# A hybrid HGRN2 and Fourier block: the heads' score products in three visits a step from second buffers, and the last head's output taken into the tail

## The chip, the cores and the metric

The kernel runs on one core of a Trainium2 chip. The metric is the device time of one execution in microseconds (us), the median of several runs. PE is the matrix engine, PEld its weight loads, DVE the vector engine, ACT the scalar engine, POOL the general engine, SP the engine that here only issues DMA transfers. A row with a q behind the engine (SPq, ACTq) is that engine's sequencer, for example when it issues a transfer.

## What is computed

One layer of a block over 2048 tokens of width 1024. After a norm with modulation, `h @ w_in` gives seven pieces of 1024 columns. Half of them feed eight heads of a recurrence that runs over the tokens forwards and backwards; the rest goes through a Fourier mixing; `w_out` joins both.

```python
k = (1.0 - lb) * jax.nn.sigmoid(-z);  log_f = jnp.log(jnp.maximum(1.0 - k, F_MIN))
...
o_inter = jnp.einsum("bhtd,bhde->bhte", qc * jnp.exp(bcum), state)
scores = jnp.einsum("bhtd,bhsd,bhtsd->bhts", qc, kc, decay)
o_intra = jnp.einsum("bhts,bhse->bhte", scores, vc)
state = state * jnp.exp(b_end)[:, :, 0, :, None] + jnp.einsum(
    "bhsd,bhse->bhde", kc * jnp.exp(b_end - bcum), vc)
...
o = o_f + flip(o_b)
out = jnp.concatenate([y_a, y_f], axis=-1) @ w_out
```

## The kernel before

Every engine has its own program, written by hand, and works it off in order; semaphores hold the engines together. There are three stages. `front` makes h, h's high and low parts (a product in float32 is three products of such parts, `mm3`, whose lines L61, L62, L63 stand for it everywhere) and the first pieces. `heads` runs eight heads. `tail` does the Fourier mixing and the output product.

In `heads` a head has NG = 4 steps (g = 0 to 3) of 512 tokens, each for both directions d = 0 and 1. Two streams of PE work are interleaved by hand in `step`:

- `project_half(h, g, slot)`, slots 0 to 9: 12 products of 128x512 each, half a tile of a piece for the next head or for this head's gates. In the last two heads only the eight slots 0, 1, 3, 4, 5, 7, 8 and 9 are filled, and in the very last step none is. I call such a half P0 to P9.
- The head's own products. The scores of a 128-token tile are made by levels, each from queries and keys that DVE has scaled for it: the first level within blocks of 8 (L1423), then the pairs of blocks of 8 and 16 (L1439), of 32 and 64 (L1452). Then the keys are transposed (L1462), the increments of the state made (L1469), and the outputs (L1478, L1479; for g = 2 and 3 both lines, for g = 0 and 1 only the second).

So PE's order in a step is P0, first level, P1 P2, level 8, P3, level 16, P4, level 32, P5, level 64, P6 P7, transposes, P8, increments, P9, outputs: the products of a head stand in eight places between halves, five of them for scores.

DVE's order in a step: `clear_scores` (L1573, g = 0 and 1), the scaling for level 8 (L1642 and L1643, with `total` L1646), `copy_scores` and `join_scores`, then for each of LEVELS = (8, 16, 32, 64) the scaling of half of the queries and keys in place (L1666, L1667, L1670) with two parts of `prepare` for the next step behind it (gates; parts 6 and 7 are the reciprocals of L1615). Then `copy_scores` of the last mask, the chain of the state (L1691, L1699), and `first_operands` of the next step (L1623 to L1629). A weight piece for the projections is split by ACT (`split_high`, L1499) and DVE (`split_low`, L1559) at places that `split_due` picks; the first piece of the next head is split after the chain of g = 3. Queries, keys and values lie in two buffers each, and SP's `load` fetches those of the next step when the step before has ended.

All scaling is in place, so DVE can scale for a level only when PE has read the level before, and PE can start a level only when DVE is through.

`tail` starts on PE with `channel_weights(0)`, `middle(0)` and `channels(0)` (L2495 and the three lines of `mm3`), for which DVE folds the loaded waves (`fold_again`, `split_fold_low`, `split_cw_low`) and ACT makes the high parts. Before ACT's first `split_p_high` it waits for the stores of the last outputs, `o_stored`. Later PE wants the third block of the Fourier rows for `f_part(2, 0, F_FIRST)`, which SP fetches by `load_f(2)` behind `load_o(0)`.

Of the kernel before, what the change touches and what calls it, by code (L numbers as in the profile page):

```python
# [35 lines left out]
P = 128  # L36
# [1123 lines left out]
class Leaving:  # L1160
# [12 lines left out]
    steps: int  # L1173


def heads(nc, block, r, front_room, work, spare, bank, handed, w_in, one_minus_lb, ident, masks, h_hi, h_lo, states, value_rows, scratch, o_rows):
# [44 lines left out]
    query = [[piece(f"query{d}{b}", at + d * row) for b, at in enumerate((VALUES + 6 * row, RAW))] for d in range(2)]  # L1221
    key = [[piece(f"key{d}{b}", at + d * row) for b, at in enumerate((HC + 6 * row, RAW + 2 * row))] for d in range(2)]
# [8 lines left out]
    score = [tiles(f"score{g}", spare + g * row) for g in range(NG)]  # L1231
# [8 lines left out]
    loaded = [[r.sem(f"loaded{d}{b}") for b in range(2)] for d in range(2)]  # L1240
    near_cleared, score_cleared = r.sem("near_cleared"), r.sem("score_cleared")
# [9 lines left out]
    key_t_copied = [r.sem(f"key_t_copied{d}") for d in range(2)]  # L1251
    o_copied = [r.sem(f"o_copied{d}") for d in range(2)]
# [3 lines left out]
    LOADS = 3  # L1256
# [15 lines left out]
    def ordered(ap, d, b):  # L1272

        return in_time(ap, d).rearrange("p (n two b) -> p n two b", two=2, b=b)

# [21 lines left out]


# [29 lines left out]
    def _(sp):  # L1328
# [5 lines left out]
        def load(h, g, parts=("key", "value", "query")):  # L1334
            for d in range(2):
                t = group_of(d, g) * GRP
                sem, b = loaded[d][g % 2], g % 2
                if "key" in parts:
                    sp.dma_start(key[d][b][:], scratch[key_names[d]][bass.ds(h * P, P), t:t + GRP]).then_inc(sem, DMA)
# [3 lines left out]
                if "query" in parts:  # L1343
                    sp.dma_start(query[d][b][:], scratch["query"][bass.ds(h * P, P), t:t + GRP]).then_inc(sem, DMA)

        def first_loads():
# [13 lines left out]
            load(0, 1, ("key", "query"))  # L1360
            sp.wait_ge(handed.product, handed.all_fills)
            load(0, 1, ("value",))
# [4 lines left out]
        def turn(h, last):  # L1367
            if h:
                start_state(h)
            for g in range(0 if h else 1, NG):  # L1370
                if g == NG - 1 and last:
                    break
                for d in range(2):
                    wait_count(sp, product[d], PROD * (NG * h + g))
                if g < NG - 1:
                    load(h, g + 1)
                else:
                    for b in range(2):
                        wait_count(sp, proj_stored[b], (FIRST_UNIT[h] // 2 + 6) * DMA)
                    load(h + 1, 0)  # L1380
# [7 lines left out]
    def _(pe):  # L1388
# [22 lines left out]
        def tile(ap, t):  # L1411
            return ap[:, t * P:(t + 1) * P]

        def step(h, g, last):
            n, b = NG * h + g, g % 2
            project_half(h, g, 0)
            for d in range(2):
                wait_count(pe, loaded[d][b], (2 * h + g // 2 + 1) * LOADS * DMA)
                wait_count(pe, operand[d], OPS * n + 1)
                for t in range(TPG):  # L1420
                    for part in PARTS:
                        for half, keys in enumerate((first_half[d], key[d][b])):
                            done = nc.tensor.matmul(half_block(ps[d][0][part, t, part], d, half), tile(keys, t)[:, part],  # L1423
                                                    half_block(tile(query[d][b], t)[:, part], d, half), start=True, stop=True)
# [1280 lines left out]
```

## Time and profile before

| | us |
|---|---|
| median of 3 runs | 2205.48 (2204.68 to 2206.7) |
| the profiled execution | 2205.83, its span 2204.1 |
| PE busy | 2114.9 |
| DVE busy | 1531.6 |
| ACT busy | 508.3 |
| heads on PE: first L1423 to last L1479 | 515.6 to 1684.4 |

The span runs from the first to the last instruction, and busy is the time in which an engine had work in it. A PE instruction is shown from its start to the end of its pipeline, so the next one starts before it ends: what a run of products costs is the distance between the starts of its first row and of the next run's first row.

### The profile page before, as it was taken

To read this page: it belongs to the slowest core of one execution; us is meant where nothing else is said; L and a number is where in the kernel's file an instruction comes from. 1 tells how busy PE (TensorE), PEld (TensorE's weight loads), DVE (VectorE), ACT (ScalarE), POOL (GpSimd) and SP (SyncE) were. 2 spreads that over 40 slices of the span, in tenths; PEclk is the share of its full clock that TensorE was granted. 3 is DMA by queue.
4 is the path that set the end of the run, shared out by engine and by line. 5 is a ranking of instruction groups with operands and counts; after the bars stand their busy time and mean duration, and the time that the engine had idled before them with its cause. 6 is when DMAs were issued, how large, how long until landed. Compare 5 with 4: busy or idle time off the path is not lost.

```text
span 2204.1 us, 48217 instructions
## 1 busy us (share of the span) xinstructions
PE 2114.9 (96%) x20564; PEld 1776.8 (81%) x20564; DVE 1531.6 (69%) x3275; ACT 508.3 (23%) x836; POOL 75.0 (3%) x109
## 2 busy tenths in 40 slices
PE   5899999999999999999999999999996999999997
PEld 3799988788788788888887887877776887888886
DVE  5865854026777878787787778798896886555554
ACT  3711133111112111212121122111112343212121
POOL 0001101000000000000000000000000010000000
PEclk9999999999999999999999999999997999999999
DMA  8444555342424333333334243333335366534451
GB/s 316 159 131 144 183 156 155 120 132 74 130 83 132 106 115 100 117 111 98 117 94 135 83 132 96 110 112 116 103 103 193 139 229 231 196 127 162 149 177 57
DMA packets 229863, 298.89 MB, mean 136 GB/s; under 512 B 14934, under 2 KB 159990, under 8 KB 226322
## 3 DMA queue, kind: packets, MB, share of 16 engines
q1 hardware_dynamic: 145346, 178.38, 25.1%
q10 hardware_dynamic: 73952, 81.18, 10.8%
q0 software_dynamic: 10352, 36.25, 5.1%
q8 instruction: 163, 2.67, 0.5%
q14 instruction: 50, 0.41, 0.1%
HBM read 198.16 MB, written 97.59 MB: 134 GB/s over the span
## 4 chain that ended last, share of the span: by engine, by line
PE 88%; DVE 5%; DMA 2%; issue 1%; ACT 1%; SPq 1%; ACTq 0%; POOL 0%; DVEq 0%
PE all_bank L61 25%; PE all_bank L63 23%; PE all_bank L62 23%; PE all_bank L1479 3%; PE all_bank L1469 2%; PE all_bank L1423 2%; PE all_bank L1439 2%; PE all_bank L1452 1%; PE all_bank L1462 1%; PE all_bank L1478 1%; DVE hidden_h_lo L483 1%; DMA front_w_mod<-in_w_ada 1%; SPq L366 1%; PE all_bank L1008 1%; PE all_bank L2566 1%
## 5 line engine op out<-in xcount | busy, mean ns | idle before, releaser
L61 PE MATMUL all_bank<-hidden_h_hi,head_hi 128*128 128x512 f32 x1184 | 491.0, 415 | 2.2 <-issue 2.2
L63 PE MATMUL all_bank<-hidden_h_hi,head_lo 128*128 128x512 f32 x1184 | 465.4, 393 | 0.0
L62 PE MATMUL all_bank<-hidden_h_lo,head_hi 128*128 128x512 f32 x1184 | 463.1, 391 | 0.0
L1515 ACT ACTIVATE head_projected<-all_bank 128x512 f32<-128x512 f32 x148 | 88.6, 599 | 864.2 <-PE all_bank L63 864.2
L63 PEld LDWEIGHTS all_bank<-hidden_h_hi,head_lo 128*128 128x128 f32 x1184 | 222.6, 188 | 51.8
L61 PEld LDWEIGHTS all_bank<-hidden_h_hi,head_hi 128*128 128x128 f32 x1184 | 222.9, 188 | 47.4 <-issue 2.5
L62 PEld LDWEIGHTS all_bank<-hidden_h_lo,head_hi 128*128 128x128 f32 x1184 | 223.4, 189 | 41.7 <-issue 2.0
L1615 DVE RECIPROCAL head_inverse<-head_gate 128x448 f32<-128x448 f32 x64 | 185.8, 2930 | 0.0
L1666 DVE TENSOR_TENSOR head_query<-head_query,head_total 128x256 f32<-128x256 f32 x256 | 107.8, 421 | 81.9 <-PE all_bank L1439 51.4
L61 PE MATMUL all_bank<-front_hi,hidden_h_hi 128*128 128x256 f32 x512 | 143.8, 281 | 0.0
L63 PE MATMUL all_bank<-front_hi,hidden_h_lo 128*128 128x256 f32 x512 | 142.7, 279 | 0.0
L62 PE MATMUL all_bank<-front_lo,hidden_h_hi 128*128 128x256 f32 x512 | 142.6, 279 | 0.0
L1667 DVE TENSOR_TENSOR head_key<-head_key,head_total 128x256 f32<-128x256 f32 x256 | 107.3, 419 | 0.0
L61 PE MATMUL all_bank<-tail_w_hi,tail_f_hi 128*128 128x512 f32 x256 | 100.6, 393 | 3.1 <-DVE tail_f_lo L2138 3.1
L61 PE MATMUL all_bank<-tail_w_hi,tail_a_hi 128*128 128x512 f32 x256 | 101.4, 396 | 1.1 <-DVE tail_a_lo L2171 1.1
L63 PE MATMUL all_bank<-tail_w_hi,tail_f_lo 128*128 128x512 f32 x256 | 100.4, 392 | 0.0
L62 PE MATMUL all_bank<-tail_w_lo,tail_f_hi 128*128 128x512 f32 x256 | 100.3, 392 | 0.0
L63 PE MATMUL all_bank<-tail_w_hi,tail_a_lo 128*128 128x512 f32 x256 | 99.9, 390 | 0.0
L62 PE MATMUL all_bank<-tail_w_lo,tail_a_hi 128*128 128x512 f32 x256 | 99.7, 389 | 0.0
L61 PEld LDWEIGHTS all_bank<-front_hi,hidden_h_hi 128*128 128x128 f32 x512 | 96.9, 189 | 0.5 <-issue 0.4
L1642 DVE TENSOR_TENSOR head_query<-head_query,head_gate 128x512 f32<-128x512 f32 x64 | 43.6, 681 | 76.8 <-PE all_bank L1423 76.8
L63 PEld LDWEIGHTS all_bank<-front_hi,hidden_h_lo 128*128 128x128 f32 x512 | 96.5, 188 | 0.0
(294 smaller groups left out, 4151.4 us busy)
## 6 DMA issues: line engine op xcount, KB each, us to landing
head_raw<-in_w_in POOLq DMA_DIRECT2D x37, 512.0 KB, 4.8
head_value<-value_rows SPq DMA_DIRECT2D x64, 256.0 KB, 5.2
head_query<-piece_query SPq DMA_DIRECT2D x64, 256.0 KB, 6.7
head_out<-head_o ACTq DMA_DIRECT2D x64, 256.0 KB, 6.1
tail_o<-head_out SPq DMA_DIRECT2D x32, 512.0 KB, 5.9
front_raw<-in_w_in SPq DMA_DIRECT2D x19, 512.0 KB, 5.1
front_stage<-in_x SPq DMA_DIRECT2D x16, 512.0 KB, 6.9
front_w_mod<-in_w_ada SPq DMA_DIRECT2D x8, 1024.0 KB, 13.6
```

Source lines behind the costliest of these rows:

```text
L61: nc.tensor.matmul(out, st_hi, mv_hi, start=start, stop=False)
L62: nc.tensor.matmul(out, st_hi, mv_lo, start=False, stop=False)
L63: return nc.tensor.matmul(out, st_lo, mv_hi, start=False, stop=stop)
L1423: done = nc.tensor.matmul(half_block(ps[d][0][part, t, part], d, half), tile(keys, t)[:, part], half_block(tile(query[d][b], t)[:, part], ...
L1439: done = nc.tensor.matmul(meeting(ps[d][BANK_OF[i]][part, t, part], d, LEVELS[i]), tile(key[d][b], t)[:, part], meeting(tile(query[d][b], ...
L1469: done = nc.tensor.matmul(ps[d][1][:, t, :], key_t[d][:, t, :], value[d][b][:, t, :], start=True, stop=True)
L1479: done = nc.tensor.matmul(ps[d][2][:, t, :], tile(query[d][b], t), state[d][:, before, :], start=g < NG // 2, stop=True)
L1515: nc.scalar.activation(projected[unit % 2][:], ps_proj[unit % 2][:], PIECES[name][1], scale=PIECES[name][2]).then_inc(proj_copied, 1)
L1615: nc.vector.reciprocal(in_blocks(inverse[d][:], d)[:, :, 1:BASE], in_blocks(gate[d][:], d)[:, :, 1:BASE]).then_inc(gated[d], 1)
L1642: nc.vector.tensor_tensor(qs, qs, f[:, :, 0:1].to_broadcast([P, GRP // BASE, BASE]), ALU.mult)
L1666: nc.vector.tensor_tensor(qs[:, :, 1, :], qs[:, :, 1, :], tot[:, :, 0, :].to_broadcast(shape), ALU.mult)
L1667: nc.vector.tensor_tensor(ks[:, :, 0, :], ks[:, :, 0, :], tot[:, :, 1, :].to_broadcast(shape), ALU.mult).then_inc(operand[d], 1)
```

## The change

In `heads`:

- Queries and keys lose their second buffer (`query[d]`, `key[d]`). The scaling for level 8 goes out of place into new tiles `query_far`, `key_far`, planes of `query_planes` and `key_planes`, by `far_operands`, which DVE runs at the end of the step before, right behind `first_operands`. Levels 8 and 16 scale these in place as before; the step to level 64 is written into the other planes (`query_turned`, `key_turned`), so it needn't wait for PE to read level 32; the step behind level 64 writes back, and four small copies on ACT (`returned`) bring back what it leaves.
- PE does the scores in three visits: first level and level 8, then level 16 behind P1 P2, then levels 32 and 64 behind P3 P4; P5 P6 P7 follow. Level 64 is made by 16 products of 32 by 64 in place of 8 of 64 by 64.
- DVE's order is changed with it, and `split_due` puts pieces due at slots 7 to 9 behind both reciprocals.
- SP issues a step's two key loads first, on semaphores of their own (`key_here`). It does so when the first level has been read and `far_operands` is through, so inside the step before.
- The last step's chain, outputs and output copies (`chain`, `outputs`, `rows_out`) are called from `tail`: the chain behind DVE's three clearing operations, the outputs behind `channel_weights(0)`, the copies behind ACT's splits of the channel weights.

In `tail`: ACT waits for `o_stored` only before the fifth `split_p_high`; `load_f(2)` is issued before `load_o(0)`, and `split_f_low(2)` comes before `add_directions(0)`.

```diff
-    query = [[piece(f"query{d}{b}", at + d * row) for b, at in enumerate((VALUES + 6 * row, RAW))] for d in range(2)]
+    query = [piece(f"query{d}", VALUES + (6 + d) * row) for d in range(2)]
...
+                    if after is not None:
+                        wait_count(sp, product[d], PROD * after + 1)
+                        wait_count(sp, operand[d], OPS * after + 2)
+                    sp.dma_start(key[d][:], scratch[key_names[d]][bass.ds(h * P, P), t:t + GRP]).then_inc(key_here[d], DMA)
...
-            project_half(h, g, 1)
-            project_half(h, g, 2)
             if n == 0:
                 pe.wait_ge(handed.evacuated, handed.all_fills)
...
+            level_in_parts(n, 0)
+            for slot in range(1, 3):
+                project_half(h, g, slot)
+            level_in_parts(n, 1)
+            for slot in range(3, 5):
+                project_half(h, g, slot)
...
+            for t in range(TPG):
+                for side in range(2):
+                    for d in range(2):
+                        done = nc.tensor.matmul(ps[d][2][PARTS[2 * d + side], t, (1 - d) * 64:(2 - d) * 64], joint_key(d)[:, 2 * t + d, side, :],
+                                                joint_query(d)[:, 2 * t + 1 - d, :, :], start=True, stop=True)
...
+                wait_count(pe, returned[d], 2 * (n + 1))
...
-                if (step, max(1, min(slot - 2, 4))) == (g, level):
+                if (step, 1 if slot < 3 else 2 if slot < 5 else 5 if slot > 6 else 4) == (g, level):
...
+        def far_operands(h, g):
+            n = NG * h + g
+            for d in range(2):
+                qs, ks, q_far, k_far, f = (in_blocks(ap, d) for ap in (query[d][:], key[d][:], query_far[d], key_far[d], gate[d][:]))
+                wait_count(v, product[d], PROD * n)
+                wait_count(v, operand[d], OPS * n + 1)
+                nc.vector.tensor_tensor(q_far, qs, f[:, :, 0:1].to_broadcast([P, GRP // BASE, BASE]), ALU.mult)
+                nc.vector.tensor_tensor(k_far, ks, f[:, :, BASE - 1:BASE].to_broadcast([P, GRP // BASE, BASE]), ALU.mult
+                                        ).then_inc(operand[d], 1)
...
             for d in range(2):
+                next_level(n, d, 0)
...
+            prepare_next(1, (0, 1))
+            for i in (1, 2):
                 for d in range(2):
...
+                    next_level(n, d, i)
+            prepare_next(2, (2, 3))
+            prepare_next(3, (4, 5))
+            for d in range(2):
+                next_level(n, d, 3)
+            prepare_next(4, (6, 7))
...
             if not ends:
                 first_operands(*next_step(h, g))
+                far_operands(*next_step(h, g))
...
+        left.chain(v, HEADS - 1, NG - 1)
...
-            sp.wait_ge(left.o_stored[d], left.steps * DMA)
+        load_f(2)
         load_o(0)
-        load_f(2)
...
+                if n == 0 and f == 4:
+                    for d in range(2):
+                        act.wait_ge(left.o_stored[d], left.steps * DMA)
                 split_p_high(n, f)
...
         channel_weights(0)
+        left.outputs(pe, HEADS - 1, NG - 1)
```

PE's order in one full step before, the first row of each run of like products (`head_query` and `head_key` are DVE's scaled operands; rows of L61 begin the projections):

```order
L1423 MATMUL all_bank6<-head_query00_5600,head_first_half0_5616 32x4x4 [waits head_operand0,head_loaded00]
...
L61 MATMUL all_bank4<-hidden_h_hi0_51,head_hi0_5594 128x512
...
L1439 MATMUL all_bank0<-head_query00_5600,head_key00_5604 32x2x8 [waits head_chained0,head_operand0]
...
L61 MATMUL all_bank5<-hidden_h_hi1_52,head_hi0_5594 128x512
...
L1439 MATMUL all_bank2<-head_query00_5600,head_key00_5604 32x16 [waits head_o_copied0,head_operand0]
...
L61 MATMUL all_bank4<-hidden_h_hi2_53,head_hi0_5594 128x512 [waits head_proj_copied]
...
L1452 MATMUL all_bank2<-head_query00_5600,head_key00_5604 32x32 [waits head_operand1,head_operand0]
...
L61 MATMUL all_bank4<-hidden_h_hi2_53,head_hi0_5594 128x512
...
L1452 MATMUL all_bank2<-head_query00_5600,head_key00_5604 64x64 [waits head_operand1,head_operand0]
...
L61 MATMUL all_bank5<-hidden_h_hi3_54,head_hi0_5594 128x512 [waits head_proj_copied]
...
L1462 MATMUL all_bank6<-all_ident,head_key00_5604 128x128 [waits head_copied0,head_operand0]
```

And the same place after the change:

```order
L1510 MATMUL all_bank6<-head_query0_5600,head_first_half0_5616 32x4x4 [waits head_operand0,head_loaded00]
...
L1497 MATMUL all_bank0<-head_query_planes0_5604,head_key_planes0_5606 32x2x8 [waits head_chained0,head_operand0]
...
L61 MATMUL all_bank4<-hidden_h_hi0_51,head_hi0_5594 128x512
...
L1497 MATMUL all_bank2<-head_query_planes0_5604,head_key_planes0_5606 32x16 [waits head_o_copied0,head_operand0]
...
L61 MATMUL all_bank5<-hidden_h_hi1_52,head_hi0_5594 128x512
...
L1527 MATMUL all_bank2<-head_query_planes0_5604,head_key_planes0_5606 32x32 [waits head_operand1,head_operand0]
...
L1536 MATMUL all_bank2<-head_query_planes0_5604,head_key_planes0_5606 32x64 [waits head_operand1,head_operand0]
...
L61 MATMUL all_bank4<-hidden_h_hi2_53,head_hi0_5594 128x512
...
L1547 MATMUL all_bank6<-all_ident,head_key_planes0_5606 128x128 [waits head_returned0,head_copied0,head_operand0]
```

The five separate places of score products have become three; L1536 is level 64, and the transposes of L1547 wait for ACT's `returned` as well.

DVE's order from the last operation of `first_operands` (L1629) into the next step, before (a step with g = 2, where nothing is cleared):

```order
L1629 TENSOR_TENSOR head_key10_5606<-head_key10_5606,head_inverse1_5615 128x64x4
L1642 TENSOR_TENSOR head_query00_5600<-head_query00_5600,head_gate0_5612 128x512 [waits head_operand0,head_product0]
L1643 TENSOR_TENSOR head_key00_5604<-head_key00_5604,head_gate0_5612 128x512
L1646 TENSOR_TENSOR head_total0_5622<-head_gate0_5612 128x64 [waits head_copied0]
L1642 TENSOR_TENSOR head_query10_5602<-head_query10_5602,head_gate1_5613 128x512 [waits head_operand1,head_product1]
L1643 TENSOR_TENSOR head_key10_5606<-head_key10_5606,head_gate1_5613 128x512
L1646 TENSOR_TENSOR head_total1_5623<-head_gate1_5613 128x64 [waits head_copied1]
L1589 COPY_PREDICATED head_near0_5624<-hidden_masks_49,all_bank6 128x512
...
L1666 TENSOR_TENSOR head_query00_5600<-head_query00_5600,head_total0_5622 128x32x8 [waits head_totalled0,head_operand0,head_product0]
```

And after the change, where L1706 is that last operation and L1714 and L1715 are `far_operands`:

```order
L1706 TENSOR_TENSOR head_key1_5603<-head_key1_5603,head_inverse1_5615 128x64x4
L1714 TENSOR_TENSOR head_query_planes0_5604<-head_query0_5600,head_gate0_5612 128x512 [waits head_operand0,head_product0]
L1715 TENSOR_TENSOR head_key_planes0_5606<-head_key0_5602,head_gate0_5612 128x512
L1719 TENSOR_TENSOR head_total0_5622<-head_gate0_5612 128x64 [waits head_copied0,head_chained0]
L1714 TENSOR_TENSOR head_query_planes1_5605<-head_query1_5601,head_gate1_5613 128x512 [waits head_operand1,head_product1]
L1715 TENSOR_TENSOR head_key_planes1_5607<-head_key1_5603,head_gate1_5613 128x512
L1719 TENSOR_TENSOR head_total1_5623<-head_gate1_5613 128x64 [waits head_copied1,head_chained1]
L1731 TENSOR_TENSOR head_query_planes0_5604<-head_query_planes0_5604,head_total0_5622 128x32x8 [waits head_totalled0,head_operand0,head_product0]
L1732 TENSOR_TENSOR head_key_planes0_5606<-head_key_planes0_5606,head_total0_5622 128x32x8
```

The scaling for level 8 stays right behind `first_operands` in DVE's order, but it now waits for the outputs of the step before instead of PE's first level of this step. The scaling for level 16 (L1731) now comes ahead of the first `copy_scores`.

SP's transfers for one step before:

```order
L1339 DMA head_key00_5604<-piece_key_f 128x512 [waits head_proj_stored0,head_proj_stored1,head_product1,head_product0]
L1341 DMA head_value00_5608<-value_rows 128x4x128
L1344 DMA head_query00_5600<-piece_query 128x512
L1339 DMA head_key10_5606<-piece_key_b 128x512
L1341 DMA head_value10_5610<-value_rows 128x4x128
L1344 DMA head_query10_5602<-piece_query 128x512
```

And after:

```order
L1417 DMA head_key0_5602<-piece_key_f 128x512 [waits head_product0,head_operand0,head_proj_stored1,head_proj_stored0]
L1417 DMA head_key1_5603<-piece_key_b 128x512 [waits head_operand1,head_product1]
L1422 DMA head_value00_5608<-value_rows 128x4x128
L1425 DMA head_query0_5600<-piece_query 128x512
L1422 DMA head_value10_5610<-value_rows 128x4x128
L1425 DMA head_query1_5601<-piece_query 128x512
```

Both keys now come first, and each waits for DVE's and PE's use of the one buffer.

## Rows read from the trace of the kernel before

**Rows 1.** The page: busy time by engine, and the chain that ended last by engine.

```profile
PE 2114.9 (96%) x20564; PEld 1776.8 (81%) x20564; DVE 1531.6 (69%) x3275; ACT 508.3 (23%) x836; POOL 75.0 (3%) x109
...
PE 88%; DVE 5%; DMA 2%; issue 1%; ACT 1%; SPq 1%; ACTq 0%; POOL 0%; DVEq 0%
```

**Rows 2.** Windows: stretch, length, busy us of each engine, granted clock, DMA share, GB/s.

```profile
1100.00:1200.00 100.00, 99.03 (x1199) 81.49 (x1199) 78.56 (x195) 19.71 (x30) 3.54 (x4) 1.00 0.34 105
1600.00:1700.00 100.00, 82.19 (x1163) 68.58 (x1161) 80.20 (x215) 17.21 (x33) 0.10 (x1) 0.89 0.39 134
1692.00:1696.00 4.00, 4.00 (x19) 3.85 (x19) 1.36 (x3) 0.82 (x3) 0.00 (x0) 0.50 1.03 427
```

**Rows 3.** Timeline of PE, third head, g = 1: start, us, instruction, count.

```profile
856.79 0.26 PE L1423 MATMUL all_bank<-head_query,head_first_half 128*32 128x16 f32 x7
...
858.18 0.50 PE L61 MATMUL all_bank<-hidden_h_hi,head_hi 128*128 128x512 f32 x1
...
863.87 0.74 PE L1439 MATMUL all_bank<-head_query,head_key 128*32 128x16 f32 x64
...
871.11 0.46 PE L1452 MATMUL all_bank<-head_query,head_key 128*32 128x32 f32 x32
871.50 0.50 PE L61 MATMUL all_bank<-hidden_h_hi,head_hi 128*128 128x512 f32 x1
...
874.46 0.69 PE L1452 MATMUL all_bank<-head_query,head_key 128*64 128x64 f32 x16
875.08 0.50 PE L61 MATMUL all_bank<-hidden_h_hi,head_hi 128*128 128x512 f32 x1
```

**Rows 4.** Timeline of PE, the same step's last projection run and its outputs.

```profile
886.03 0.48 PE L61 MATMUL all_bank<-hidden_h_hi,head_hi 128*128 128x512 f32 x1
...
890.02 1.24 PE L1479 MATMUL all_bank<-head_state,head_query 128*128 128x128 f32 x9 [0.97 <-DVE head_state L1699]
```

**Rows 5.** Timeline of DVE, the same step: a wait inside it.

```profile
883.04 1.23 DVE L1559 TENSOR_TENSOR head_lo<-head_raw,head_hi 128x1024 fp32r<-128x1024 f32 x1 [3.42 <-ACT head_hi L1499]
```

**Rows 6.** Timeline of DVE, third head, from g = 0 into g = 1.

```profile
848.75 0.35 DVE L1699 SCALAR_TENSOR_TENSOR head_state<-head_state,head_total,all_bank 128x128 f32<-128x128 f32 x1 [1.60 <-issue]
...
854.33 0.43 DVE L1629 TENSOR_TENSOR head_key<-head_key,head_inverse 128x256 f32<-128x256 f32 x1
...
857.66 0.69 DVE L1642 TENSOR_TENSOR head_query<-head_query,head_gate 128x512 f32<-128x512 f32 x1 [1.82 <-PE all_bank L1423]
...
860.27 0.27 DVE L1646 TENSOR_TENSOR head_total<-head_gate 128x64 f32<-128x64 f32 x1
```

**Rows 7.** Timeline of DVE, from the sixth head into the seventh.

```profile
1424.43 1.23 DVE L1559 TENSOR_TENSOR head_lo<-head_raw,head_hi 128x1024 fp32r<-128x1024 f32 x1 [2.96 <-ACT head_hi L1499]
...
1428.45 0.43 DVE L1629 TENSOR_TENSOR head_key<-head_key,head_inverse 128x256 f32<-128x256 f32 x1
```

**Rows 8.** Timeline of PE: starts of the first level in heads seven and eight.

```profile
1428.67 0.26 PE L1423 MATMUL all_bank<-head_query,head_first_half 128*32 128x16 f32 x7
...
1463.79 0.26 PE L1423 MATMUL all_bank<-head_query,head_first_half 128*32 128x16 f32 x7
...
1495.07 0.26 PE L1423 MATMUL all_bank<-head_query,head_first_half 128*32 128x16 f32 x7
...
1660.56 0.26 PE L1423 MATMUL all_bank<-head_query,head_first_half 128*32 128x16 f32 x7
```

**Rows 9.** DMA issues: queue, count, KB each, median us from issue to landing.

```profile
head_key<-piece_key_b SPq DMA_DIRECT2D x32, 256.0 KB, 5.9
```

**Rows 10.** Timeline of PE at the start of the tail and at its third Fourier block.

```profile
1690.94 0.38 PE L2475 MATMUL all_bank<-tail_cw,tail_mid_in 128*1 128x256 f32 x1 [3.67 <-DVE tail_cw_lo L2089]
...
1701.63 0.58 PE L61 MATMUL all_bank<-tail_cw_hi,tail_fold_hi 128*128 128x256 f32 x1 [4.00 <-DVE tail_mid_lo L2094]
...
1840.76 0.47 PE L61 MATMUL all_bank<-tail_w_hi,tail_f_hi 128*128 128x512 f32 x1 [2.81 <-DVE tail_f_lo L2138]
```

**Rows 11.** Timeline of ACT at the start of the tail.

```profile
1700.76 0.37 ACT L2385 ACTIVATE tail_mid_hi<-all_bank 1x256 fp32r<-1x256 f32 x1 [7.83 <-issue]
```

More of the change, by code:

```diff
@@ L1255, in heads @@
     key_names = ("key_f", "key_b")
-    LOADS = 3
+    LOADS = 2
     def meeting(ap, d, size):
@@ L1458, in step @@
+            for slot in range(5, 8):
+                project_half(h, g, slot)
             for d in range(2):
@@ L1471, in step @@
             project_half(h, g, 9)
-            for d in range(2):
-                wait_count(pe, copied[d], MASKED * n + MASKED)
-                wait_count(pe, chained[d], CHAIN * n + TPG)
-                for t in range(TPG):
-                    before = t if d == 0 else TPG - 1 - t
-                    if g >= NG // 2:
-                        nc.tensor.matmul(ps[d][2][:, t, :], score[group_of(d, g)][:, t, :], value[d][b][:, t, :], start=True, stop=False)
-                    done = nc.tensor.matmul(ps[d][2][:, t, :], tile(query[d][b], t), state[d][:, before, :], start=g < NG // 2, stop=True)
-                done.then_inc(product[d], 1)
+            if not (last and g == NG - 1):
+                outputs(pe, h, g)
         pe.wait_ge(handed.sig_done, HEADS)
@@ L1649, in step, with prepare_next @@
                 v.wait_ge(handed.masks_in, DMA)
+            def prepare_next(level, parts):
+                due = split_due(h, g, level)
+                if not ends:
+                    prepare(*next_step(h, g), parts[0])
+                if due is not None:
+                    split_low(h, due)
+                if not ends:
+                    prepare(*next_step(h, g), parts[1])
             for d in range(2):
+                next_level(n, d, 0)
+            for d in range(2):
+                wait_count(v, product[d], PROD * n + 1)
                 if g < NG // 2:
@@ L2378, in _ @@
         nc.scalar.activation(sign_row[:], raw_sign_row[:], ACT.Copy).then_inc(signs_ready, 1)
-        for d in range(2):
-            act.wait_ge(left.o_stored[d], left.steps * DMA)
         for n in range(FG):
@@ L2389, in _ @@
             for f in range(8):
+                if n == 0 and f == 2:
+                    for sem in left.proj_stored:
+                        act.wait_ge(sem, left.all_units // 2 * DMA)
+                if n == 0 and f == 4:
+                    for d in range(2):
+                        act.wait_ge(left.o_stored[d], left.steps * DMA)
                 split_p_high(n, f)
```

281 lines of the change are left out of this document (168 added, 113 removed).

## The prediction

> **What bounds the kernel now.** I read the page first. PE is busy for 2114.9 of 2204.1 us and makes up 88% of the chain that ended last, DVE 5% [rows 1]. So only what shortens PE's own stream, or an idle stretch of it, counts. The windows say where idle time is: in a hundred microseconds of the middle heads PE is busy for 99.03, in the hundred that end the heads for 82.19, at a mean granted clock of 0.89 [rows 2]. So in the middle heads the change can gain only by cheaper PE work, and at the end by removed waits too.
>
> The timeline of PE shows what a visit costs. A lone half of 12 products between two visits takes 874.46 - 871.50 = 2.96 us; two halves in a row take 863.87 - 858.18 = 5.69 [rows 3]. From 2.96 and 5.69, a half that only lengthens a run costs 2.73, and each break adds about 0.22.
>
> The same timeline has one wait that recurs: at g = 1 of heads one to six the projections ahead of the outputs take 890.02 - 886.03 = 3.99 us, because PE waits for the chain of the state [rows 4]. DVE is late there since it stood 3.42 us for ACT's high part of a weight piece, with one reciprocal still to do [rows 5].
>
> In heads seven and eight, with eight halves a step, DVE becomes the limit. The seven steps before the last take 1660.56 - 1428.67 = 231.9 us. The second, which has no PE wait at its scores, takes 1495.07 - 1463.79 = 31.28 [rows 8].
>
> **The change part by part.**
>
> *Fewer visits.* Of the runs P1 P2, P3, P4, P5, P6 P7 (2 x 5.69 + 3 x 2.96 = 20.26) there remain P1 P2, P3 P4, P5 P6 P7: 5.69 + 5.69 + 8.42 = 19.80. Two breaks fewer: 0.44 a step after rounding down. I take 0.44 x 31 = 13.6 us; the last step has no halves. That more work in a row saves nothing bounds it at 0.
>
> *Level 64.* It takes 875.08 - 874.46 = 0.62 us for 16 rows of 64x64; afterwards 32 rows with 32 columns of weights and 64 moving. Level 32, with the same number of rows and the same 32-column weights but half the moving columns, takes 871.50 - 871.11 = 0.39 [rows 3]. So the new level 64 lies between 0.39 and twice that, 0.78: from 0.23 gained to 0.16 lost a step. Four column groups now run side by side as in level 32, so I take 0.52, a gain of 0.1, 3 us in all, with -5 to +7 as ends.
>
> The first level shows the pace of small products: 128 rows in 858.18 - 856.79 = 1.39 us, 10.9 ns each [rows 3]. The Trainium skill, "TensorE: Matmul & The Clock Gate", section "Part 1: The HAM clock gate", says that the start-to-start distance never drops below about 25 ns however few columns there are. By that 32 rows would take 0.8 us, and level 64 would lose 0.18 a step, 5.6 us in all. The row is less than half of that floor here, so the measurement decides.
>
> *The wait at g = 1.* The piece that waits for ACT now comes behind both reciprocals. DVE then loses only what exceeds them (2.9 us of the 3.42 are covered), and before the chain it has 1.60 us to spare at g = 0 [rows 5, 6]. So the six waits go: 3.99 - 2.96 = 1.03 each, 6 us.
>
> *Level 8 right behind the first level.* Its cover, P1 P2, is gone; what is late next is `far_operands`. At g = 0 DVE ends the last operation of `first_operands` at 854.76, 2.03 before PE's first level at 856.79 [rows 3, 6]. `far_operands` is L1642 to L1646 for both directions: 860.54 - 857.66 = 2.9 us [rows 6]. Started at 854.7 it ends at 857.5, while the second direction's level 8 is wanted at 856.79 + 1.39 + 0.3 = 858.5. That leaves about 0.9 of cover, more at g = 2, where the outputs are 32 rows and not 16. If this cover is missing, each microsecond costs one at every step.
>
> It is missing at the seven boundaries between heads. There DVE waits 2.96 us for ACT before it splits the next weight piece, and ends `first_operands` at 1428.88 [rows 7]; `far_operands` would follow to 1431.8, its last key operand to about 1431.6. PE starts the first level at 1428.67 [rows 8] and would want the second level 8 at 1430.4, 1.2 earlier. That is a new loss of 7 x 1.2 = 8, less 1 that level 8 waits there already: 7 us lost.
>
> *Heads seven and eight.* With no waits, the seven steps would take four times 31.28, three times 33.2 (two microseconds more for the double outputs), less 2.96 because the last of them is not followed by P0: 221.8. So 10 us are waits for level 8, whose operands DVE makes too late. They are ready early now. DVE's own work is some 28.5 us a step, so it follows closely. I leave 2 us for levels 32 and 64, which are now wanted together. Gain 8, between 4 and 10; the boundaries' loss is booked above.
>
> *Keys.* They are fetched inside the step: SP issues about 0.8 and 1.4 us after the first level starts. The second key's median landing is 5.9 us behind two other transfers [rows 9], with one ahead I take 4.6. So both are there 6 us into the step, when DVE has cleared, scaled level 16 and copied twice. Behind DVE's wait for them stand the scalings for levels 32 and 64. With ten halves level 64 is wanted at 14.3, and key plus two parts, a weight split and two scalings need 6.1 us: 2 us of cover. With eight halves it is wanted at 11.8, and 5.0 are needed: 0.8 of cover. Cost nothing. ACT's four copies lie under P5 P6 P7.
>
> *Last step and tail.* In the last step PE only follows DVE and ACT. Its order saves about a microsecond. The chain's tail end then lies under `channel_weights(0)`. PE's `middle(0)` waited 3.67 us at 1690.94 for folds that DVE started behind the chain, with ACT busy with the output copies ahead of its splits; both come earlier now. `channels(0)` then stood 4.00 us up to 1701.63, because ACT had waited 7.83 us for stores to land before its first high part [rows 10, 11]. That wait moves to the fifth part. Meanwhile PE worked at a granted clock of 0.50, which is its 1.2 GHz level [rows 2]. Sum of 1 + 3.67 + 4.00 is 8.7; the stores may still be late for the fifth part, so I take 8, from 3 (only the first wait) to 11 (with time back from the clock).
>
> *Third Fourier block.* PE waited 2.81 us [rows 10]. Its load is issued three transfers earlier; but the first heads' rows then land later, and the turning of heads follows. 2.5 gained, 0 to 3.
>
> **Sum.** 13.6 + 3 + 6 - 7 + 8 + 8 + 2.5 = 34.1 us off the profiled 2205.83, which is 0.35 above the median 2205.48. Off the median it gives 2171.4, and I say 2171.
>
> **The rivals.**
> - *Forecast,* 2171, own range 2160 to 2182.
> - *The cover of level 8 is not there at g = 0 to 2 either.* If `far_operands` ends 1 us later than the 0.9 of cover allows, 24 further steps lose 1 each: 2171 + 24 = 2195. For it: DVE's chain hardly moves while PE's step shrinks. Against it: at g = 0 DVE still waits 1.60 us before the chain [rows 6].
> - *Breaks cost what they did,* since level 8 and the longer runs bring their own start-up: no 13.6, so 2185. Against it are the two runs of [rows 3].
> - *Small products keep to a floor.* Level 64 then takes 0.8: 2171 + 3 + 5.6 = 2180.
> - *Slower: late keys.* If the second key landed 8.9 us after its issue, 3 above the median, it would be there 10.3 into the step. Level 64 is then late by 2.1 in 12 steps, by 1 in 12 without a split, and by 3.5 in 7 of eight halves: 25 + 12 + 25 = 62, so 2233. It outweighs the gain from about 7.5 us after issue on. For it: one buffer, and the output stores are in flight. Against it: the median, and that keys go first.
>
> **How the numbers follow.** Forecast 0.64; level 8 exposed 0.14; breaks not saved 0.09; floor 0.03; late keys 0.06; the gains just eaten up by small losses in several places 0.04. The range 2158 to 2193 takes in the first, third and fourth, and a part of the second (the cover missed by less). A difference under 0.2%, 4.4 us, can't be told from no change here. Faster: 0.64 + 0.14 + 0.09 + 0.03, less 0.01, is 0.89; same 0.04; slower 0.07.
>
> **What would show it.** After: two halves in a row at 5.7 and P5 P6 P7 at 8.4 us; level 64 at 0.5; no 3.99 at g = 1; a PE wait of some 1.2 before level 8 only where a head begins; DVE's first part of `prepare` hardly waiting for keys; `middle(0)` some 5 us sooner after the last step's first level, and no 4 us wait in `channels(0)`. The prediction is wrong if waits at level 8 stand in every step, if L1673 waits for DMA for more than 2 us, or if PE's wait for `f_part(2, 0, F_FIRST)` only moves to the heads' turning.

## The result and the profile after

| | before | after |
|---|---|---|
| median, side by side | 2206.19 us (2204.68 to 2208.93) | 2212.14 us (2206.21 to 2218.65) |
| runs | 8 | 8 |
| the profiled execution, its span | 2205.83, 2204.1 | 2210.46, 2208.7 |

The ratio is 1.0029, with a 95% interval of 1.0015 to 1.0043. The kernel became slightly slower. The forecast was 2171, so some 40 us are missing.

The page after answers to [rows 1]:

```profile
PE 2105.5 (95%) x21076; PEld 1784.5 (81%) x21076; DVE 1531.3 (69%) x3275; ACT 537.2 (24%) x964; POOL 74.9 (3%) x109
...
PE 87%; DVE 5%; issue 3%; DMA 2%; ACT 2%; SPq 1%; ACTq 0%; DVEq 0%
```

PE's busy time fell by 9.4 us and the span rose by 4.6. The share "issue", time in which PE waited for nothing that the profile shows, rose from 1% to 3%. DVE and DMA kept theirs, ACT went from 1% to 2%.

I read the timeline of PE in several steps of the changed kernel. This is the third head's g = 2, it answers to [rows 3] (L1497 is level 8, then level 16; L1527 is level 32, L1536 level 64; the first level began 1.27 us earlier). Each float32 product of the code's levels stands there as two rows, and the counts in this text are of rows:

```profile
868.23 0.74 PE L1497 MATMUL all_bank<-head_query_planes,head_key_planes 128*32 128x16 f32 x63
868.89 0.51 PE L61 MATMUL all_bank<-hidden_h_hi,head_hi 128*128 128x512 f32 x1
...
874.61 0.74 PE L1497 MATMUL all_bank<-head_query_planes,head_key_planes 128*32 128x16 f32 x64
875.28 0.51 PE L61 MATMUL all_bank<-hidden_h_hi,head_hi 128*128 128x512 f32 x1
...
881.00 0.46 PE L1527 MATMUL all_bank<-head_query_planes,head_key_planes 128*32 128x32 f32 x32
881.27 0.68 PE L1536 MATMUL all_bank<-head_query_planes,head_key_planes 128*32 128x64 f32 x32
881.88 0.50 PE L61 MATMUL all_bank<-hidden_h_hi,head_hi 128*128 128x512 f32 x1
...
890.24 1.04 PE L1547 MATMUL all_bank<-all_ident,head_key_planes 128*128 128x128 f32 x8
```

Here all is as planned. Two halves in a row take 874.61 - 868.89 = 5.72, three take 890.24 - 881.88 = 8.36. Levels 32 and 64 together take 881.88 - 881.00 = 0.88, against 0.39 + 0.62 = 1.01 in [rows 3]. Level 8 follows the first level without a pause.

In about half the steps something else happens. Three of them:

```profile
980.68 0.25 PE L1497 MATMUL all_bank<-head_query_planes,head_key_planes 128*32 128x16 f32 x7
984.34 0.95 PE L1497 MATMUL all_bank<-head_query_planes,head_key_planes 128*32 128x16 f32 x57 [3.41 <-issue]
985.22 0.80 PE L61 MATMUL all_bank<-hidden_h_hi,head_hi 128*128 128x512 f32 x1
985.81 0.63 PE L62 MATMUL all_bank<-hidden_h_lo,head_hi 128*128 128x512 f32 x1
...
1025.51 0.45 PE L1497 MATMUL all_bank<-head_query_planes,head_key_planes 128*32 128x16 f32 x32 [1.92 <-issue]
...
1103.99 0.40 PE L61 MATMUL all_bank<-hidden_h_hi,head_hi 128*128 128x512 f32 x1 [1.86 <-issue]
```

Level 8 is 64 rows, and its semaphores are waited for ahead of each direction's 32. PE stopped for 3.41 us behind the 7th row, where the code has no wait at all, and elsewhere behind the last one. There it can be no late operand. Ahead of its last step the heads' stage has 15 such stops in the changed kernel. From the start of the product ahead to the start of the one behind they last 1.38 to 3.59 us, 35.7 in all. The longest also slow what follows, as the windows show (columns as in [rows 2]):

```profile
984.00:986.00 2.00, 1.66 (x59) 1.53 (x59) 1.07 (x4) 0.00 (x0) 0.00 (x0) 0.50 0.92 279
986.00:988.00 2.00, 2.00 (x7) 1.52 (x6) 2.00 (x6) 0.00 (x0) 0.00 (x0) 0.50 0.92 296
988.00:990.00 2.00, 2.00 (x6) 1.60 (x5) 1.24 (x4) 0.00 (x0) 0.00 (x0) 0.50 0.06 18
```

After the pause the granted clock is 0.50, the 1.2 GHz level, and the next two halves take 8.2 us instead of 5.7. So they do behind the stops at 517.30, 670.64 and 1291.42 as well (8.1 to 8.3 us).

The expected wait where a head begins, and the tail:

```profile
832.03 0.45 PE L1497 MATMUL all_bank<-head_query_planes,head_key_planes 128*32 128x16 f32 x32 [0.94 <-DVE head_key_planes L1715]
...
1702.82 0.59 PE L2591 MATMUL all_bank<-tail_cw,tail_mid_in 128*1 128x256 f32 x2 [1.13 <-DVE tail_cw_lo L2199]
1710.01 0.35 PE L61 MATMUL all_bank<-tail_cw_hi,tail_fold_hi 128*128 128x256 f32 x1 [0.65 <-DVE tail_p_lo L2209]
...
1826.64 0.50 PE L61 MATMUL all_bank<-tail_w_hi,tail_f_hi 128*128 128x512 f32 x1 [0.67 <-DVE tail_f_lo L2248]
```

The boundary wait is 0.94 us of idle time, and 1.1 us from start to start (I had said 1.2). The waits of 3.67, 4.00 and 2.81 us of [rows 10] are 1.13, 0.65 and 0.67 now.

**What the stops share.** PE's instructions come by a DMA queue of their own. The page has it before and after (packets, MB, share of the span):

```profile
q8 instruction: 163, 2.67, 0.5%
```

```profile
q8 instruction: 167, 2.74, 0.5%
```

I counted PE's instructions in the program, a weight load and a product for each row, and one more for each wait that is an instruction of its own: 41,814 before and 42,838 after. Divided by 163 and 167 packets that is 256.5 in each. So PE is fed in blocks of 256. I then numbered the instructions and looked up the first one behind each stop (seven of the 15 are shown):

```
after:  at us     stop   number   mod 256      before: at us     stop   number   mod 256
        517.30    3.23    7106    194                  1433.54   2.51   30146    194
        670.64    2.82   10946    194                  1499.95   2.34   31938    194
        712.68    1.71   11971    195                  1568.15   2.35   33730    194
        750.78    2.12   12995    195                  1633.13   1.78   35522    194
        980.75    3.59   18882    194
       1101.94    2.04   21954    194
       1617.62    1.96   35522    194
```

All 15 of after and all 4 of before stand at 194 to 196 modulo 256: a block's end. In the trace the packet that ends such a stop starts 2.2 to 2.8 us ahead of its end.

This gives **theory 1**. The next block is asked for about when PE enters one, and takes some microseconds to come: at the 15 stops of after, 3.0 to 5.1 us lie between PE's first instruction of a block and its first one of the next, at the 4 of before 6.1 to 6.6. The first level is 256 instructions in 1.3 us, level 8 is 128 in 0.67. Put back to back, they can hold a whole block, which is used up in 1.3 us. The blocks' ends drift by 16 to 52 instructions a step in heads one to six, therefore some steps stop and others don't. **Theory 2**: VectorE's `far_operands` are late and the profile misattributes it. **Theory 3**: the key, value and query loads, now issued just then, hold something up.

Theory 1 needs one correction, which the same trace gives. PE used up six other blocks of the changed kernel in 1.2 to 2.5 us, from 630.3, 941.1, 1212.6, 1251.8, 1483.0 and 1677.9 on, and stopped for 0.7 us at most at their ends. This is the second of them, the first level's 256 instructions and level 8 behind them without a pause:

```profile
941.08 0.26 PE L1510 MATMUL all_bank<-head_query,head_first_half 128*32 128x16 f32 x7
...
942.47 0.73 PE L1497 MATMUL all_bank<-head_query_planes,head_key_planes 128*32 128x16 f32 x64
```

If the packets carry the blocks in order, the packet with the next block had started 2.2 to 2.9 us ahead of PE's first instruction of the block in five of the six (0.03 behind it in the last). At the 15 stops it started 0.6 to 2.6 us behind that instruction. The 15 blocks begin 10 to 137 instructions behind a step's first small product; of the six, one begins 6 behind it and the others with it or up to 11 ahead. So the next block isn't always asked for when PE enters one: what counts is how long ahead its packet starts. In none of the nine traces does PE begin a block less than 2.2 us behind the start of its packet.

The Trainium skill, "Runtime: NRT & Kernel Launch", section "Instruction fetch mechanics", states that an engine's instruction memory is refilled in 16 KiB blocks of 256 instructions and calls the cost of crossing such a boundary mostly hidden. The block size agrees with the 256.5 counted here. That it is hidden holds for most of this program, but not for these 35.7 us.

### The profile page after: what moved, and what is told of

It reads as the page before. It is cut to its first block, busy times and chain, and to the rows that moved or that the text cites. A ratio compares the mean times of both kernels' runs of the same rounds, so it can differ in the third digit from the quotient of the medians.

```text
span 2208.7 us, 49593 instructions
## 1 busy us (share of the span) xinstructions
PE 2105.5 (95%) x21076; PEld 1784.5 (81%) x21076; DVE 1531.3 (69%) x3275; ACT 537.2 (24%) x964; POOL 74.9 (3%) x109
## 4 chain that ended last, share of the span: by engine, by line
PE 87%; DVE 5%; issue 3%; DMA 2%; ACT 2%; SPq 1%; ACTq 0%; DVEq 0%
PE all_bank L61 25%; PE all_bank L63 24%; PE all_bank L62 23%; PE all_bank L1554 3%; PE all_bank L1345 2%; PE all_bank L1497 2%; PE all_bank L1510 2%; PE all_bank L1547 1%; PE all_bank L1344 1%; DVE hidden_h_lo L483 1%; PE all_bank L1536 1%; PE all_bank L1008 1%; PE all_bank L2682 1%; DMA front_w_mod<-in_w_ada 1%; SPq L366 1%
## 5 line engine op out<-in xcount | busy, mean ns | idle before, releaser
L61 PE MATMUL all_bank<-hidden_h_hi,head_hi 128*128 128x512 f32 x1184 | 488.3, 412 | 2.8 <-issue 2.8
L63 PE MATMUL all_bank<-hidden_h_hi,head_lo 128*128 128x512 f32 x1184 | 470.4, 397 | 0.3 <-issue 0.2
L61 PEld LDWEIGHTS all_bank<-hidden_h_hi,head_hi 128*128 128x128 f32 x1184 | 226.1, 191 | 47.5 <-issue 0.7
L61 PE MATMUL all_bank<-front_hi,hidden_h_hi 128*128 128x256 f32 x512 | 143.6, 281 | 0.0
L1372 DVE SCALAR_TENSOR_TENSOR head_state<-head_state,head_total,all_bank 128x128 f32<-128x128 f32 x256 | 71.8, 343 | 85.8 <-issue 72.1
L1731 DVE TENSOR_TENSOR head_query_planes<-head_query_planes,head_total 128x256 f32<-128x256 f32 x128 | 53.8, 420 | 75.8 <-PE all_bank L1497 60.3
L61 PE MATMUL all_bank<-tail_w_hi,tail_a_hi 128*128 128x512 f32 x256 | 102.1, 399 | 3.0 <-DVE tail_a_lo L2281 3.0
L61 PE MATMUL all_bank<-tail_w_hi,tail_f_hi 128*128 128x512 f32 x256 | 99.9, 390 | 0.7 <-DVE tail_f_lo L2248 0.7
L61 PEld LDWEIGHTS all_bank<-front_hi,hidden_h_hi 128*128 128x128 f32 x512 | 96.7, 189 | 0.5 <-issue 0.4
L62 PEld LDWEIGHTS all_bank<-front_lo,hidden_h_hi 128*128 128x128 f32 x512 | 96.2, 188 | 0.0
```

Source lines behind the costliest of these rows:

```text
L61: nc.tensor.matmul(out, st_hi, mv_hi, start=start, stop=False)
L62: nc.tensor.matmul(out, st_hi, mv_lo, start=False, stop=False)
L63: return nc.tensor.matmul(out, st_lo, mv_hi, start=False, stop=stop)
L1372: nc.vector.scalar_tensor_tensor(state[d][:, j + 1, :], state[d][:, j, :], total_of(d, P)[:, j:j + 1], ps[d][1][:, t, :], ALU.mult, ALU.ad ...
L1731: nc.vector.tensor_tensor(qs, qs, tot[:, :, 0, :].to_broadcast(shape), ALU.mult)
```

## The experiments

**1 and 2. The same program, with its blocks' ends moved.** Waits that are met since long before are instructions as well. Put between projection products they make each step a multiple of 256 long. Nothing is left out or reordered.

```diff
+        def fill(h, g, n, k):
+            first = sum(map(len, SLOTS_OF[h][:g])) + 2
+            places = 4 * (len(SLOTS_OF[h][g]) - 2)
+            at = 4 * (n - first) + k % 4
+            if at >= 0:
+                few = FILL[NG * h + g] * (at + 1) // places - FILL[NG * h + g] * at // places
+                for _ in range(few + 1 if few else 0):
+                    pe.wait_ge(lo_done, 1)
...
             for k in range(half * KT // 2, (half + 1) * KT // 2):
+                fill(h, g, n, k)
                 done = mm3(nc, ps_proj[unit % 2][:], ...
```

The two kernels have the same `FILL` except for step 0, whose entry is 479 in the first and 240 in the second. `FILL` counts calls of `wait_ge`, and by the traces two calls make one instruction: step 0 has 255 instructions more than in the changed kernel in the first and 128 in the second. That sets where a block ends in the later steps: 185 to 191 or 56 to 62 instructions behind the first small product.

> The changed kernel with waits that are always met added ahead of TensorE's projection products, so that every step of the heads holds a multiple of 256 TensorE instructions and the places 194 mod 256 of its program fall about 185 instructions behind each step's first small product (step 0 excepted). Theory 1, TensorE's instructions arrive in blocks of 256 and a block that is used up in under some 4 us leaves it without the next: the stalls of 1.7 to 3.6 us between two products of L1497 go, except that of step 0; 35.7 less 3.2 us of stalls and about 8 us of halved clock behind the longest: 2171 us. Theory 2, VectorE's operands for level 8 come late: nothing in the data's order is changed, the stalls stay, 2212 us. Theory 3, the loads that SyncE now issues just there hold something up: the same, 2212 us.

Measured: 2177.03 us (4 runs), ratio to before 0.9863, interval 0.985 to 0.9877.

> As the first of this set, with 127 to 129 added waits fewer in step 0 and the same ones in every later step, so that the places 194 mod 256 fall about 62 instructions behind each step's first small product. Theory 1: a block of 256 lies wholly in the first level and level 8 in each of the 31 steps behind step 0, each stalls about 2.1 us as the steps with such an offset did in the changed kernel: 2171 + 31 x 2.1 = 2236 us, with all stalls at one place of the step. Theories 2 and 3: no difference to the first of this set, 2212 us or the time that it has.

Measured: 2274.67 us (4 runs), ratio 1.0314, interval 1.0294 to 1.0333. The groups of level 8 and 16 in the two, first the one with the good place:

```profile
L1509 PE MATMUL all_bank<-head_query_planes,head_key_planes 128*32 128x16 f32 x4096 | 49.1, 185 | 12.2 <-DVE head_key_planes L1727 6.6 <-issue 5.0 <-DVE head_key_planes L1744 0.6
```

```profile
L1509 PE MATMUL all_bank<-head_query_planes,head_key_planes 128*32 128x16 f32 x4096 | 57.2, 188 | 70.2 <-issue 69.7 <-DVE head_key_planes L1744 0.3
```

The idle time put down to "issue" is 5.0 us in one and 69.7 in the other. Three steps of the second:

```profile
845.99 0.75 PE L1509 MATMUL all_bank<-head_query_planes,head_key_planes 128*32 128x16 f32 x37 [3.32 <-issue]
...
886.43 0.57 PE L1509 MATMUL all_bank<-head_query_planes,head_key_planes 128*32 128x16 f32 x37 [1.81 <-issue]
...
1374.23 0.57 PE L1509 MATMUL all_bank<-head_query_planes,head_key_planes 128*32 128x16 f32 x37 [1.97 <-issue]
```

In these, 37 rows of level 8 are left each time. Every step from 1 to the last stops at a number of 194 or 195 modulo 256. Data, order of the work, operands and loads are the same in both kernels, which lie 98 us apart. That rules theories 2 and 3 out as the cause and bears theory 1 out. I had put the bad one 39 us too low. The 32 stops make 78.9 us, 2.5 each and not 2.1. In 12 steps of heads one to six the next two halves took 6.95 to 8.23 us instead of 5.7, where I had counted no clock at all:

```profile
846.00:850.00 4.00, 4.00 (x45) 3.29 (x45) 3.67 (x11) 0.00 (x0) 0.00 (x0) 0.50 0.82 259
```

The good one missed 2171 by 6 us, in step 0: it took 47.1 us there, with a stop of 3.45, then the clock at half, and 255 added waits to pay for.

**3. The kernel before with filled steps.** The same `fill`.

> The kernel before with the same filling of its steps, places 194 mod 256 about 185 behind each step's first small product. Theory 1: its four stalls between products of level 8 in heads 7 and 8 (2.51, 2.34, 2.35 and 1.78 us at 1433.54, 1499.95, 1568.15 and 1633.13) go, 9.0 us: 2197 us. Theory 2, these four are waits for VectorE, as the prediction booked them: 2206 us. Against the first of this set it tells what the rest of the change is worth when neither kernel stalls for instructions: 26 us by theory 1.

Measured: 2212.0 us, ratio 1.002, interval 1.0011 to 1.0029: a miss, by 15 us. The stops of 2.3 us in level 8 of heads seven and eight did go. This is one in the kernel before, then two of what stands in the filled one:

```profile
1436.05 0.18 PE L1439 MATMUL all_bank<-head_query,head_key 128*32 128x16 f32 x1 [2.32 <-issue]
```

```profile
1440.86 0.47 PE L61 MATMUL all_bank<-hidden_h_hi,head_hi 128*128 128x512 f32 x1 [0.72 <-issue]
...
1474.37 0.47 PE L61 MATMUL all_bank<-hidden_h_hi,head_hi 128*128 128x512 f32 x1 [0.87 <-issue]
```

The block's end now falls into the projections behind level 8, with only 2.9 us of them between the two levels, and steps there stop for up to 1.3 us from start to start, where before every second one stopped for 1.8 to 2.5. In these seven steps PE's idle time put down to "issue" is 5.2 us in all, and 3.7 more are waits for ACT's copies of the projections, which before didn't have. The filling costs too: heads one to six, which had no long stop, take 3.3 us more in all, and the part from the last step on 3.2 more, for which I have no cause. So four stops of before were waits for instructions, not for VectorE, but filling alone gives nothing back there.

**4. The part behind the heads alone.** The last step's outputs, rows and chain in the stage behind, its splits and loads in the new order, on the kernel before:

```diff
             project_half(h, g, 9)
-            for d in range(2):
-                wait_count(pe, copied[d], MASKED * n + MASKED)
...
+            if not (last and g == NG - 1):
+                outputs(pe, h, g)
```

> The kernel before with the part of the change behind the last head alone (the last step's outputs, rows and chain moved into the stage behind, the order of its splits and loads). If the gain there is independent of the heads, it is the 12 us by which the stretch from the last step's first level to the end is shorter in the changed kernel: 2194 us. If that gain depends on the new buffers or on what the heads leave behind: between 2194 and 2206 us.

Measured: 2194.6 us, ratio 0.9946, interval 0.9933 to 0.9958. This part gives 12 us by itself.

**5. Level 8 behind slots 1 and 2 again,** with nothing filled:

```diff
-            level_in_parts(n, 0)
             for slot in range(1, 3):
                 project_half(h, g, slot)
+            level_in_parts(n, 0)
+            project_half(h, g, 3)
             level_in_parts(n, 1)
-            for slot in range(3, 5):
-                project_half(h, g, slot)
+            project_half(h, g, 4)
```

> The changed kernel with level 8 behind slots 1 and 2 again, slot 3 behind level 8, slot 4 behind level 16, nothing filled up: four visits to the scores instead of three. Theory of the instruction blocks: 5.7 us of projections lie between the 256 instructions of the first level and the 128 of level 8 in heads 1 to 6, so the 40 us of stalls and halved clock there go; heads 7 and 8, with 2.9 us between, keep some of what the kernel before had (up to 9 us); one visit more costs 31 x 0.22 = 7 us, and the waits of 0.94 us at the seven boundaries of heads go, 7 us: 2212 - 40 + 9 + 7 - 7 = 2181 us. If the three visits were worth nothing, the time is no longer than the 2177 us of the filled three visits.

Measured: 2251.81 us, ratio 1.02, interval 1.0179 to 1.0221: a miss of 71 us. The stops for instructions are nearly gone, but a real wait took their place:

```profile
898.06 0.46 PE L1527 MATMUL all_bank<-head_query_planes,head_key_planes 128*32 128x32 f32 x32 [0.89 <-DVE head_key_planes L1732]
899.57 0.65 PE L1536 MATMUL all_bank<-head_query_planes,head_key_planes 128*32 128x64 f32 x31 [1.05 <-DVE head_key_planes L1737]
```

By groups, level 32 stood 26.8 us for VectorE and level 64 stood 31.6. The clock takes its part too: in 12 steps the three halves behind level 64 took 9.4 to 10.1 us instead of 8.4, some 18 us in all, with windows like this one:

```profile
900.00:904.00 4.00, 4.00 (x26) 3.10 (x16) 4.00 (x14) 0.91 (x4) 0.00 (x0) 0.57 0.02 5
```

In the changed kernel both are wanted 5.7 us behind level 16, here 3.0. Level 8 right behind the first level is what makes room for two halves between the others. It can't be moved back alone.

**6 and 7. The filled kernel with step 0 put right.** The front's last products get met waits as well, so that in step 0 a block ends 192 instructions behind the first small product. In the second, heads seven and eight use other slots:

```diff
+FRONT_FILL = [4, 4, 4, 4, 4, 4, 3, 3]
...
                 for k in range(KT):
+                    if n == NB - 1 and f >= 2:
+                        for _ in range(FRONT_FILL[k]):
+                            pe.wait_ge(lo_done, 1)
                     last = mm3(nc, bank[n_fill % 4][:, u * W:(u + 1) * W], a_hi[:, k, at], a_lo[:, k, at],
```

```diff
-    EIGHT = (0, 1, 3, 4, 5, 7, 8, 9)
+    EIGHT = (0, 1, 2, 3, 5, 7, 8, 9)
```

> The changed kernel filled to 256 in every step, as the run that took 2177 us, and 196 or so met waits added to the last products of the front too, so that step 0 has its block's end at 192 as well and needs no 255 of them itself. Theory of the instruction blocks: the stall of 3.45 us in step 0 goes and some 7 us of halved clock and of filling there: 2167 us. If step 0's loss was due to the start of the stage: 2177 us.

Measured: 2168.63 us, ratio 0.9824, interval 0.9809 to 0.984. Step 0 takes 36.1 us instead of 47.1.

> As the run before it, with the eight slots of heads 7 and 8 as 0, 1, 2, 3, 5, 7, 8, 9 instead of 0, 1, 3, 4, 5, 7, 8, 9: 24 projection products behind level 8 and 12 behind level 16. Theory of the instruction blocks: the stalls of about 1 us behind level 8 in heads 7 and 8 (three in the first filled run) go: 3 us less than the run before it, 2164 us. Against it: VectorE must have level 32 and 64 ready behind 2.9 us of projections instead of 5.7, and is late: slower than the run before it by up to 7 x 2 us.

Measured: 2166.75 us, ratio 0.9822, interval 0.9808 to 0.9837: no difference to the run before it that these runs can tell. The short stops in heads seven and eight went ("issue" idle 0.3 us there instead of 1.0), and level 64 waited for VectorE five times there, 0.9 us in all, where it had not waited before. Both kernels beat the two given ones by about 40 us. One stop is left in each, in the last step, which has no projections (the second's):

```profile
1641.99 0.75 PE L1515 MATMUL all_bank<-head_query_planes,head_key_planes 128*32 128x16 f32 x34 [4.64 <-issue]
```

PE's stretches, from first products to first products, in us:

| | step 0 | rest of heads 1 to 6 | heads 7, 8 but the last step | from the last step on |
|---|---|---|---|---|
| before | 36.8 | 876.3 | 231.9 | 543.5 |
| changed | 41.7 | 894.9 | 226.4 | 530.3 |
| 1, good place | 47.1 | 859.2 | 222.8 | 534.8 |
| 2, bad place | 39.5 | 933.1 | 247.6 | 535.3 |
| 6 | 36.1 | 859.3 | 222.3 | 532.9 |

## Why the prediction was wrong

**The step that failed** is "Level 8 right behind the first level". I asked there whether DVE would have the operands in time, and priced PE's small products by their pace alone. How PE's own instructions reach it was no term of the sum. The change put 384 of them into 2.0 us. That cost 35.7 us of stops and some 12 of halved clock behind them. Ahead of the last step the changed kernel's heads took 1163.0 us and those of experiment 6 1117.7, 45.3 less, its added waits included. This turned the gain of 34 into a loss of 6. Experiments 1 and 2 show it: the same work at the good place is 35 us faster than the changed kernel, at the bad place 63 slower.

**A reading that failed** is "Heads seven and eight". I took all of the 10 us above the pace of a step without waits as level 8 waiting for DVE. The rows say "<-issue", in the middle of a run of products. Four stops make up 9.0 of them, and all four stand at a block's end. That the term of 8 came out close (231.9 to 222.3 in experiment 6, 9.6) is luck, since its reason was wrong. The warning stood in the profile of before: the two levels with only 2.9 us between them stopped 2.3 us, in heads seven and eight alone. I should have asked what these steps have that others lack.

**Terms that held.** They can be read once the stops are gone, in experiment 6:
- Visits: two halves at 5.7, three at 8.4; 0.46 a step, 0.44 as put.
- Level 64: 0.13 a step with level 32, forecast 0.1. The rival's 0.8 us for the 32 rows didn't come: they took 0.61 us, 19 ns each.
- g = 1: the wait is gone in all six heads.
- Boundaries: 0.94 us idle and 1.1 from start to start, where I had 1.2. The first level is also 0.1 us shorter in each step, 3 to 4 us in all, which I hadn't counted.
- Heads in all: 1145.0 before, 1117.7 in experiment 6, 27.3 gained. The sum had 23.6 (34.1 less 8 and 2.5). Of the 27.3, 17.7 lie in heads one to six and 9.6 in seven and eight.
- Last step and tail: 12 us alone (experiment 4), forecast 10.5.

With its instructions in time the change takes 2168.6 us, near the 2171 of the forecast. Part of this nearness is luck too: 9.0 us of the gain are the kernel before's own four stops, which the sum had under another name.

**The rivals.** The cover of level 8, breaks and the floor did not come true. The late keys did not either: in the changed kernel `prepare` (L1673) waited 3.7 us for keys in all, of which 2.9 were ahead of the first step and 0.8 inside the heads. Level 64 stood for VectorE once, for 0.8 us, in the last step, which has no projections. By its letter one sign of being wrong was met, a wait of L1673 for DMA above 2 us; the wait of 2.1 lies at 484.2, 31 us ahead of PE's first level of the first head. "Slower" had 0.07 of the chance, and none of that lay on the mechanism that made it slower.

## What to carry to other kernels

- Count TensorE's instructions as well as their time. In experiment 2 a block of 256 lay wholly in small products in all 31 steps behind step 0, and all 31 stopped. With some 4 us of work in a block, four steps of heads seven and eight of the kernel before stopped and others of the same kernel didn't. And blocks that began just ahead of the small products were used up in 1.2 to 2.5 us without a long stop. So look at where in the stretch a block begins. Keeping the two short runs apart by long products cost more here (experiment 5); moving the blocks' ends by filling paid off in the changed kernel (1 and 6), not in the one before (3).
- "<-issue" in the middle of a run whose code has no wait there is a reading of its own. Look at the distance from start to start and at the instruction's number in the program before you book it as a late operand.
- If a change makes some steps slower and their equals not, compare where in the program, not only in the step, they stand.

## What the runs showed of the hardware

- TensorE's instructions arrived in blocks of 256 (163 packets for 41,814, 167 for 42,838). The stops ended 2.2 to 2.8 us behind the start of their packet, and in all nine traces no block was begun sooner than that behind its packet's start, if packets carry blocks in order. Between PE's first instruction of a block and its first of the next lay 3.0 us at the quickest stop (712.7) and 7.3 at the slowest (experiment 6, in the last step, where PE also waits for VectorE); 6.1 to 6.6 at the four stops of before. The difference goes with how late the packet started: 0.6 us behind PE's first instruction of the block at 712.7, 3.6 to 4.4 behind it at the four of before. What sets the packet's start is open.
- Two kernels that do the same work in the same order differed by 98 us of 2200, by where the program's blocks end.
- The stops of 2.8 to 3.6 us in the changed kernel were followed by a granted clock of 0.50. The stop of 3.51 us in step 0 of experiment 2 was not, as its window shows, and behind stops of 2 us it differed from step to step (two halves at 5.7 or at 7.3 us in experiment 2).

```profile
519.00:523.00 4.00, 1.19 (x6) 0.97 (x6) 3.63 (x11) 0.00 (x0) 0.00 (x0) 1.00 0.97 276
```

- Waits that are already met cost nothing that shows when one or two instructions of them stand ahead of three 512-column products, nor with four, in heads seven and eight of experiment 6 (two halves at 5.7 us). Eight ahead of each three, in step 0 of experiment 1, were part of a stretch of 7.2 us instead of 5.7.
- Products with 32 columns of weights and 16 moving were issued every 10 ns, so 5 ns an instruction (first level, 128 rows in 1.27 us): a block lasts 1.3 us at this pace.
